# Quadrant score products, rearranged fp32 products and split first loads in a two-layer decoder step

## Chip, core and metric

One core of a Trainium2 chip runs the whole kernel. The metric is the device time of one execution in microseconds (us), lower is better. The profile shows five engines: PE (TensorE: matmul, with PEld for its weight loads), DVE (VectorE), ACT (ScalarE), POOL (GpSimd) and SP (the queue that issues the DMAs).

## What is computed

One inference step of a two-layer decoder trunk on a prompt of 2048 tokens (width 1024) and on 8 single tokens ("samples"). Layer 0 has a gated linear recurrence (RG-LRU) and layer 1 a sliding-window attention with 16 heads of 64 over a window of 128 keys; both have, beside it, a 4-head attention over a memory of 256 rows. Cut to what matters:

```python
mem_n = rmsnorm(mem_prompt[None], mem_norm_g[:, None, None, :])
mkv = jnp.einsum('lbmd,lde->lbme', mem_n, w_mem_kv)          # memory K and V of both layers
for l in range(2):
    proj = rmsnorm(x, norm_g[l]) @ w_in[l]
    u, g_main, q_mem, g_mem = split(proj)
    y = rglru(causal_conv(u)) if l == 0 else sink_attend(rope(u), k_att, v_att, band_mask, sinks)
    om = mem_attend(q_mem, mem_k[l], mem_v[l])
    x = x + concat(y * silu(g_main), om * silu(g_mem)) @ w_out[l]

def band_mask(nb):                                            # of 256 keys, query qi sees 128
    qi = jnp.arange(WINDOW)[:, None] + WINDOW
    ki = jnp.arange(2 * WINDOW)[None, :]
    local = (ki <= qi) & (qi - ki < WINDOW)
```

Everything is float32. The large products are made from three products of split operands (hi*hi, hi*lo, lo*hi) in the type fp32r; small ones (memory K/V, samples, transposes, scores and values of the window attention, the gates of the recurrence) are plain fp32 matmuls, which the profile shows as two records each (transposes as one).

## The kernel before

Each engine runs a list of instructions written out by hand, and semaphores tie the lists together. The order on PE is therefore the order in the code.

**Start** (`start`). SP loads the parameters `prm`, the transposed memory `mem_T` and the samples `xs_T` (both into `mt`, semaphore `mm_ld`), then the memory's weights `w[0]` and `w[1]` (`mk_ld`), the prompt's chunk 0 once as rows (`xr`, for the sums of squares) and once as columns (`raw`), and so on. ACT scales the memory by its gain (`memory_gain`, one step for each of 8 parts k of the width), squares it and then the rows of chunk 0 (`squares`), and takes roots. DVE adds up the squares (`tree`), inverts the roots and builds diagonal matrices (`diagonal`). PE makes the memory's products `memory(i)`, i = 0 to 3 for layer 0 (16 matmuls each, two halves h times eight parts k), `memory_sums`, and the factors as products with a diagonal: `memory_spread` for the memory, `spread(c)` for chunk c of the prompt. Its order is memory 0, sums, memory 1, memory_spread, spread 0, memory 2, memory 3. DVE then normalizes the chunk (`normal`), ACT rounds it (`high`), DVE forms the rest (`low`); `evac(i)` takes the memory's products out of PSUM.

**Memory attention** (`mem_pe`, 16 items per layer: 4 heads by 4 chunks c of 512 tokens). For item q PE does two projections of 24 matmuls (`project` for query and gate, line 569), the transposes of the item before (`mem_flip`, line 649), the scores (`mem_scores`, line 674), the values of the item before (`mem_values`, lines 661 and 664); in an item with c = 1 the samples' projection (`project_samples`, line 589, 8 matmuls with 32 stationary columns), and in layer 0's items 2, 6, 10 and 14 the memory's products 4 to 7 of layer 1 (`end`, which calls `memory`, line 414). The weights of `memory(4)` are loaded by `load_second` once `spread(3)` of item 2 is done.

**Recurrence** (`lru_pe`, 32 items): project, gates of the item before (`lru_gates`, line 861: four 64x64 matmuls on the four quadrants of the array), project, and with q % 4 = 1 the samples' projection.

**Window attention** (`swa_pe`, 32 items): project, transposes of item q-2 (`swa_flip`, line 1096), scores of item q-1 (`swa_scores`, line 1112: 8 matmuls, for four tiles t of 128 queries and two heads h; head h lies in partitions 64h to 64h+63), project, values of item q-2 (`swa_values`, line 1123), with q % 4 = 0 the samples' projection. ACT copies the second 128 keys' scores to `X`; DVE replaces the columns k > q of `X` by those of the first 128 keys (`swa_max`, by the predicate `pick`), so of the 256 scores of a query 128 are used.

**Output projection** (`output`, line 1970) follows in each layer.

Of the kernel before, what the change touches and what calls it, by code (L numbers as in the profile page):

```python
# [8 lines left out]
ACT = mybir.ActivationFunctionType  # L9
# [4 lines left out]
KT = D // 128  # L14
# [11 lines left out]
M = 256  # L26
# [118 lines left out]
def start(nc, m, sem, A, outs):  # L145
# [3 lines left out]
    prm_ld, sink_ld, ids, soft, exp_r = (sem("su_" + s) for s in ("prm", "sink", "ids", "soft", "exp"))  # L149
    mm_ld, mm_g, mm_sq, mm_add, mm_sum, mm_rt, mm_dg, mm_bc, mm_xs = (sem("mm_" + s) for s in ("ld", "g", "sq", "add", "sum", "rt", "dg", "bc", "xs"))  # L150
    mk_ld = [sem(f"mk_ld{i}") for i in range(8)]
    mk_kt = [sem(f"mk_kt{p}") for p in range(2)]
    mk_done, mk_ev, mk_st = (sem("mk_" + s) for s in ("done", "ev", "st"))
    x_ld, r_ld = ([sem(f"in_{n}{c}") for c in range(NCH)] for n in ("ld", "rows"))
# [36 lines left out]
    def sync(s, item_weights):  # L191
        def load_rows(c):
            s.dma_start(xr[c][:, :, :], A["x_prompt"][0, CH * c:CH * c + CH].rearrange("(t p) d -> p t d", p=128)).then_inc(r_ld[c], 16)

        def load_columns(c):
            s.dma_start(raw[c][:, :, :], A["x_T"][c]).then_inc(x_ld[c], 16)

        def load_x(c):
            load_rows(c)
            load_columns(c)  # L200

        def load_w(i):
            s.dma_start(w[i][:, :, :], A["w_mem_kv"][i]).then_inc(mk_ld[i], 16)

        s.dma_start(m.prm[:, :, :], A["prm"]).then_inc(prm_ld, 16)
        s.dma_start(mt[:, :, 0:M], A["mem_T"]).then_inc(mm_ld, 16)
        s.dma_start(mt[:, :, M:NM], A["xs_T"]).then_inc(mm_ld, 16)
        load_w(0)
        load_w(1)
        load_x(0)  # L210
        load_w(2)
        load_w(3)
        item_weights(s, 0)
        load_x(1)
        load_x(2)
        item_weights(s, 1)

        s.wait_ge(mk_done, 2)
        load_rows(3)
        s.wait_ge(mk_done, 4)  # L220
        load_columns(3)
        s.dma_start(m.sink_bc[:, :], A["sinks"].broadcast_to([128, NH])).then_inc(sink_ld, 16)
        for b in range(NS):
            s.dma_start(m.sink_col[b * NH:(b + 1) * NH, :], A["sinks"].rearrange("a h -> h a")).then_inc(sink_ld, 16)
        for i in range(4):
            store(s, i)
# [53 lines left out]
            nc.scalar.activation(m.hi[c][:, half(h), :], raw[c][:, half(h), :], ACT.Copy).then_inc(x_hi, 1)  # L280

    def scalar(act, first_weights):
        def memory_gain(l):
            for k in range(KT):
                nc.scalar.activation(mg[l][k][:, :], mt[:, k, 0:M], ACT.Copy, scale=m.prm[:, k, R_MG + l:R_MG + l + 1]).then_inc(mm_g, 1)

        act.wait_ge(prm_ld, 16)
        act.wait_ge(mm_ld, 32)
        memory_gain(0)
        nc.scalar.activation(sqm[:, :, :], mt[:, :, :], ACT.Square).then_inc(mm_sq, 1)  # L290
        act.wait_ge(ids, 2)
        squares(act, 0)
        act.wait_ge(mm_sum, 1)
        nc.scalar.activation(st[:, 12:14], sums_m[:, 0:2], ACT.Sqrt, bias=m.eps, scale=1.0 / D)
        nc.scalar.activation(st[0:NS, 14:15], sums_m[0:NS, 2:3], ACT.Sqrt, bias=m.eps[0:NS, :], scale=1.0 / D).then_inc(mm_rt, 1)
        memory_gain(1)
        high(act, 0)
        first_weights(act)
        squares(act, 1)
# [39 lines left out]
    def vector(v, c, first_weights):  # L339
        v.wait_ge(mm_sq, 1)  # L340
        tree(v, c, sqm, mm_add)
        v.wait_ge(ids, 8)
        c.link(nc.vector.tensor_tensor(m.twin[:, :], m.ident[:, 0:NS], m.ident[:, NS:2 * NS], ALU.add))
        for j in range(1, 4):
            c.link(nc.vector.tensor_tensor(m.twin[:, :], m.twin[:, :], m.ident[:, 32 * j:32 * j + NS], ALU.add))
        diagonal(v, c, 0)
        v.wait_ge(mm_rt, 1)
        c.link(nc.vector.reciprocal(st[0:NS, 18:19], st[0:NS, 14:15]))
        c.link(nc.vector.reciprocal(rows_m, st[:, 12:14]))
        nc.vector.tensor_tensor(dgm[0:NS, 2, 0:NS], m.ident[0:NS, 0:NS], st[0:NS, 18:19].broadcast_to([NS, NS]), ALU.mult)  # L350
        nc.vector.tensor_tensor(dgm[:, 0:2, :], m.ident[:, :].unsqueeze(1).broadcast_to([128, 2, 128]), bc(rows_m, 128), ALU.mult).then_inc(mm_dg, 1)
        normal(v, 0)
        v.wait_ge(mm_bc, 1)
        c.link(nc.vector.tensor_copy(rbm[:, :], factor_m))
        evac(v, 0)
        evac(v, 1)
        low(v, 0)
        evac(v, 2)
        first_weights(v)

        y = mt[:, :, M:NM]
        c.link(nc.vector.tensor_tensor(y, y, rbm[:, M:NM].unsqueeze(1).broadcast_to([128, KT, NS]), ALU.mult))
        c.link(nc.vector.tensor_copy(m.xs[:, :, 0:NS], y))
        nc.vector.tensor_tensor(m.xs[:, :, NS:2 * NS], y, m.xs[:, :, 0:NS].bitcast(F32), ALU.subtract)
        nc.vector.tensor_tensor(m.xsg[:, :, 0:NS], y, bc(m.prm[:, :, R_G], NS), ALU.mult).then_inc(mm_xs, 1)
        diagonal(v, c, 1)
        evac(v, 3)
# [34 lines left out]

    def memory(pe, i):
        l = i // 4
        pe.wait_ge(mk_ld[i], 16)
        if i >= 4:
            pe.wait_ge(mk_ev, i)
        for h in range(2):
            for k in range(KT):
                if h == 0 and i % 4 == 0:  # L410
                    pe.wait_ge(mm_g, KT * l + k + 1)
                a, b = w[i][:, k, :], mg[l][k][:, :]
                s_, r_ = (a[:, 128 * h:128 * h + 128], b) if is_k(i) else (b[:, 128 * h:128 * h + 128], a)
                last = nc.tensor.matmul(mk_bank(i)[:, 256 * h:256 * h + 256], s_, r_, start=(k == 0), stop=(k == KT - 1))  # L414
        last.then_inc(mk_done, 1)

    def tensor(pe):
        def memory_sums():
            pe.wait_ge(mm_add, 1)
            for t in range(3):  # L420
                n = 128 if t < 2 else NS
                last = nc.tensor.matmul(m.bank[2][0:n, 8 * t:8 * t + 8], sqm[:, 0, 128 * t:128 * t + n], ones[:, 0:8], start=True, stop=True)
            last.then_inc(mm_sum, 1)

        def memory_spread():
            pe.wait_ge(mm_dg, 1)
            nc.tensor.matmul(factor_m[:, 0:M], ones[:, :], dgm[:, 0:2, :].rearrange("p t c -> p (t c)"), start=True, stop=True)
            nc.tensor.matmul(factor_m[:, M:NM], ones[0:NS, :], dgm[0:NS, 2, 0:NS], start=True, stop=True).then_inc(mm_bc, 1)

        pe.wait_ge(ids, 1)  # L430
        memory(pe, 0)
        memory_sums()
        memory(pe, 1)
        memory_spread()
        spread(pe, 0)
        memory(pe, 2)
        memory(pe, 3)

    return dict(exponential=exponential, sync=sync, pool=pool, scalar=scalar, vector=vector, softplus=softplus, softplus_in=softplus_in, tensor=tensor,
# [4 lines left out]
def items(nc, m, sem, l, A, st, prior=None):  # L444
# [300 lines left out]
    def mem_pe(pe, ready=None, within=None, values=None, samples=None, end=None):  # L745
        for q, (i, p, c) in enumerate(MEM):
            project(pe, "mem", i, p, 0, c, ready if q < NCH else None)
            if within:
                within(pe, q)
            project(pe, "mem", i, p, 1, c)  # L750
            if q:
                mem_flip(pe, *MEM[q - 1])
            mem_scores(pe, i, p, c)
            if q:
                if values:
                    values(pe, q)
                mem_values(pe, *MEM[q - 1])
            if q == 0 and l == 0:
                project_samples(pe, "mem", 0)
            if c == 1:  # L760
                if samples:
                    samples(pe, q)
                of_samples(project_samples, pe, "mem", i, p)
            if end:
                end(pe, q)

    def mem_act(act, within, behind=None, flipped=None):
        for q, (i, p, c) in enumerate(MEM):
# [96 lines left out]
    def lru_pe(pe, tail):  # L865
        for q in range(NL + 1):
# [6 lines left out]
            else:  # L873
                tail(pe)
                lru_gates(pe, q - 1)
            if q < NL:
                project(pe, "main", *LRU[q][:2], 1, q % 4)
            if q == 0:
                mem_values(pe, *MEM[-1])
            if q < NL and q % 4 == 1:  # L880
                of_samples(project_samples, pe, "main", *LRU[q][:2])

    def lru_tanh(act, chn, q):
        i, p, c = LRU[q]
# [214 lines left out]
    def swa_scores(pe, q):  # L1099
# [4 lines left out]
        else:  # L1104
# [2 lines left out]
            pe.wait_ge(S["zeros"], B["zeros"] + 2)  # L1107
            pe.wait_ge(S["k_ready"], B["k_ready"] + NCH)
            pe.wait_ge(S["v_ready"], B["v_ready"] + NCH)
        for t in range(4):  # L1110
            for h in range(2):
                last = nc.tensor.matmul(m.bank[2 + 2 * h + t // 2][:, (t % 2) * 256:(t % 2 + 1) * 256],  # L1112
                                        qf[q % 2][64 * h:64 * h + 64, t * 128:(t + 1) * 128],
                                        kT[64 * h:64 * h + 64, (4 * c + t) * 128:(4 * c + t + 2) * 128], start=True, stop=True)
        last.then_inc(S["s_done"], 1)

    def swa_values(pe, q):
# [1224 lines left out]
```

## Time and profile before

| | |
|---|---|
| time, median of 3 runs | 2135.05 us (2134.81 to 2135.98) |
| time of the profiled execution | 2137.04 us |
| its span, first to last instruction | 2135.1 us |
| PE busy | 2110.6 us, 99% of the span |
| DVE busy | 1148.2 us, 54% |
| ACT busy | 924.2 us, 43% |
| DMA, mean over the span | 94 GB/s; 388 GB/s in the first fortieth |
| PE in `project` (line 569), output (line 1970) | 48% and 23% of the chain that ended last |

The chain that ended last is followed back from the last instruction, at each step to what released it. Busy time of PE counts an instruction from its start to its modelled end, so that it also covers short stalls inside it; what a block costs is better read from the distance of starts in the chain.

### The profile page before, as it was taken

What the parts mean: (1) busy time and instruction counts of PE and PEld (TensorE: products, weight loads), DVE (VectorE), ACT (ScalarE), POOL (GpSimd) and SP (SyncE); (2) the same over time, 40 slices, a digit from 0 to 9 for tenths busy, and PEclk for the clock granted to TensorE, in tenths of its full rate; (3) what the DMA queues carried; (4) which work ended last, traced back from release to release, by engine and by line L of the source; (5) the groups of instructions that cost most, each with busy time, mean ns of one, the idle gap of its engine ahead of it and who ended that gap; (6) DMA issues with size and microseconds to landing.
All of it is one profiled execution on the core that took longest, in us unless ns stands there. A gap on an engine that the chain in (4) does not pass through costs nothing.

```text
span 2135.1 us, 28239 instructions
## 1 busy us (share of the span) xinstructions
PE 2110.6 (99%) x11357; PEld 1690.5 (79%) x11357; DVE 1148.2 (54%) x2016; ACT 924.2 (43%) x2012; POOL 26.8 (1%) x30
## 2 busy tenths in 40 slices
PE   7999999999999999999999999999999999999998
PEld 6788887777777787888788888888888888787886
DVE  4745436777767722222644544777767777723222
ACT  5633335777777732222533333444444344322111
POOL 0000000000000000000400000000000000000000
PEclk9999999999999999999999999999999999999999
DMA  9311111111112565243111102221222214475331
GB/s 388 121 62 40 67 54 49 45 49 44 49 44 71 178 205 172 93 125 108 63 35 37 43 35 65 75 67 48 77 73 68 65 58 134 132 271 174 104 104 56
DMA packets 114521, 199.91 MB, mean 94 GB/s; under 512 B 12252, under 2 KB 66844, under 8 KB 109392
## 3 DMA queue, kind: packets, MB, share of 16 engines
q1 hardware_dynamic: 114392, 198.13, 27.7%
q8 instruction: 89, 1.46, 0.3%
q14 instruction: 40, 0.33, 0.0%
HBM read 149.68 MB, written 48.48 MB: 93 GB/s over the span
## 4 chain that ended last, share of the span: by engine, by line
PE 91%; DVE 4%; ACT 2%; DMA 1%; issue 0%; SPq 0%; DVEq 0%
PE bank L569 48%; PE bank L1970 23%; PE bank L1112 3%; PE bank L1123 3%; PE bank L414 3%; PE bank L674 2%; PE bank L861 1%; PE bank L1096 1%; PE bank L661 1%; PE bank L649 1%; PE bank L589 1%; PE bank L664 1%; PE bank L1958 1%; DVE in_x L323 1%; DVE wo_lo L1712 1%; PE bank L1433 0%
## 5 line engine op out<-in xcount | busy, mean ns | idle before, releaser
L569 PE MATMUL bank<-x_hi,w_hi 128*128 128x512 f32 x1600 | 638.8, 399 | 1.2 <-ACT it_kraw L619 1.2
L569 PE MATMUL bank<-x_hi,w_lo 128*128 128x512 f32 x1600 | 624.1, 390 | 0.0
L569 PE MATMUL bank<-x_lo,w_hi 128*128 128x512 f32 x1600 | 623.4, 390 | 0.0
L569 PEld LDWEIGHTS bank<-x_hi,w_hi 128*128 128x128 f32 x1600 | 300.1, 188 | 110.4 <-issue 49.5
L569 PEld LDWEIGHTS bank<-x_hi,w_lo 128*128 128x128 f32 x1600 | 300.3, 188 | 64.7
L569 PEld LDWEIGHTS bank<-x_lo,w_hi 128*128 128x128 f32 x1600 | 300.6, 188 | 59.9 <-issue 0.7
L1970 PE MATMUL bank<-wo_hi,z_hi 128*128 128x512 f32 x768 | 303.1, 395 | 2.1 <-DVE z_lo L1741 2.1
L1970 PE MATMUL bank<-wo_hi,z_lo 128*128 128x512 f32 x768 | 299.2, 390 | 0.0
L1970 PE MATMUL bank<-wo_lo,z_hi 128*128 128x512 f32 x768 | 299.1, 389 | 0.0
L1970 PEld LDWEIGHTS bank<-wo_hi,z_hi 128*128 128x128 f32 x768 | 144.2, 188 | 35.3 <-DVE z_lo L1741 3.0
L1970 PEld LDWEIGHTS bank<-wo_hi,z_lo 128*128 128x128 f32 x768 | 144.2, 188 | 30.4
L1159 ACT ACTIVATE it_X<-it_X,stat 128x128 f32<-128x128 f32 x256 | 99.2, 389 | 157.3 <-DVE stat L1229 157.3
L1970 PEld LDWEIGHTS bank<-wo_lo,z_hi 128*128 128x128 f32 x768 | 144.3, 188 | 28.7
L614 ACT ACTIVATE it_gh<-bank 128x512 f32<-128x512 f32 x96 | 56.8, 592 | 173.3 <-PE bank L569 173.3
L720 DVE TENSOR_TENSOR it_P_lo<-bank,it_P_hi 128x512 fp32r<-128x512 f32 x64 | 41.2, 687 | 161.1 <-ACT it_P_hi L715 161.1
L1741 DVE TENSOR_TENSOR z_lo<-z_raw,z_hi 128x1536 fp32r<-128x1536 f32 x32 | 56.2, 1758 | 101.1 <-ACT z_hi L1737 101.1
L1195 DVE TENSOR_TENSOR it_PTs<-bank,tmask 128x512 f32<-128x512 f32 x128 | 79.5, 684 | 54.7 <-PE bank L1096 54.7
L1907 ACT ACTIVATE op_y<-op_x 128x1024 f32<-128x1024 f32 (+1 forms) x18 | 19.1, 1059 | 192.9 <-DVE op_x L1927 192.9
L1737 ACT ACTIVATE z_hi<-z_raw 128x1536 fp32r<-128x1536 f32 x32 | 47.6, 1487 | 98.8 <-DMA z_raw<-z_scratch 98.8
L709 ACT ACTIVATE it_Pm<-bank,stat 128x256 f32<-128x256 f32 x128 | 58.9, 474 | 70.6 <-DVE stat L727 70.5
L1927 DVE TENSOR_TENSOR op_x<-op_x,bank 128x512 f32<-128x512 f32 (+1 forms) x36 | 24.5, 685 | 114.2 <-PE bank L1970 114.1
L547 ACT ACTIVATE w_hi<-w_raw,prm 128x256 fp32r<-128x256 f32 x200 | 85.0, 506 | 0.3 <-PE bank L664 0.3
(308 smaller groups left out, 2694.6 us busy)
## 6 DMA issues: line engine op xcount, KB each, us to landing
w_raw<-in_w_items SPq DMA_DIRECT2D x25, 1024.0 KB, 5.0
z_scratch<-it_gz SPq DMA_DIRECT2D x96, 256.0 KB, 2.5
z_raw<-z_scratch SPq DMA_DIRECT2D x32, 768.0 KB, 5.7
it_cs<-in_rope SPq DMA_DIRECT2D x32, 512.0 KB, 4.2
wo_raw<-in_w_out SPq DMA_DIRECT2D x6, 2048.0 KB, 9.0
mk_w<-in_w_mem_kv SPq DMA_DIRECT2D x8, 1024.0 KB, 7.0
in_rows<-in_x_prompt SPq DMA_DIRECT2D x4, 2048.0 KB, 28.9
in_x<-in_x_T SPq DMA_DIRECT2D x4, 2048.0 KB, 26.5
```

The costliest lines, as they stand in the source:

```text
L414: last = nc.tensor.matmul(mk_bank(i)[:, 256 * h:256 * h + 256], s_, r_, start=(k == 0), stop=(k == KT - 1))
L547: nc.scalar.activation(m.w_hi[w % 2][:, k, :], m.w_raw[w % 2][:, k, :], ACT.Copy, scale=m.prm[:, k, gain(w):gain(w) + 1]).then_inc(S["w_hi ...
L569: last = nc.tensor.matmul(ps, s_, r_, start=(k == 0 and q == 0), stop=(k == KT - 1 and q == 2))
L614: nc.scalar.activation(gh[:, :], PG, ACT.Copy, scale=0.5)
L709: nc.scalar.activation(Pm[:, t, :], (S0, S1)[t // 2][:, (t % 2) * M:(t % 2 + 1) * M], ACT.Exp, bias=negm[:, t:t + 1], scale=MEM_SCALE, acc ...
L1112: last = nc.tensor.matmul(m.bank[2 + 2 * h + t // 2][:, (t % 2) * 256:(t % 2 + 1) * 256], qf[q % 2][64 * h:64 * h + 64, t * 128:(t + 1) * ...
L1123: last = nc.tensor.matmul(T0[64 * h:64 * h + 64, t * 128:(t + 1) * 128], kV[:, 4 * c + t + kt, 64 * h:64 * h + 64], PTs[:, h, kt, t * 128: ...
L1159: e = nc.scalar.activation(X[:, j, :], X[:, j, :], ACT.Exp, bias=negm[:, j:j + 1], accum_out=rs[:, j:j + 1])
L1195: r = nc.vector.tensor_tensor(PTs[:, h, a, :].rearrange("p (t k) -> p t k", t=4), (T0, T1)[h].rearrange("p (t k) -> p t k", t=4), m.tmask[ ...
L1737: nc.scalar.activation(m.z_hi[slot(t)][:, :, :], m.z_raw[slot(t)][:, :, :], ACT.Copy).then_inc(zhi, 1)
L1741: nc.vector.tensor_tensor(m.z_lo[slot(t)][:, :, :], m.z_raw[slot(t)][:, :, :], m.z_hi[slot(t)][:, :, :].bitcast(F32), ALU.subtract).then_i ...
L1970: last = nc.tensor.matmul(bank(t, h)[0:128 if t < TT else 40, :], s_, r_, start=(first and q == 0), stop=(end and q == len(pairs) - 1))
```

## The change

The window scores are cut in four: the 128 queries of a tile become two halves r, each multiplied with the 192 keys that it can see, so that 16 matmuls of 64 stationary and 192 moving columns stand in place of 8 of 128 and 256, on the quadrants (rows of head h, columns of half r). In the memory attention the samples' projection (in layer 0 from item 5 on) and `end` stand directly behind the transposes, ahead of the scores. In the recurrence the samples' projection stands behind the gates, ahead of the gate's projection. At the start the first loads are cut in halves of k, `xs_T` is loaded behind `w[0]`, ACT issues one small activation before it waits for data and scales the first four k when their half is there; PE does memory 0, memory 1, sums, spread 0, memory 2, memory_spread, memory 3; DVE does `low(0)` before it takes over the memory's factors.

```diff
--- before.py
+++ after.py
@@ -149,6 +149,8 @@
     prm_ld, sink_ld, ids, soft, exp_r = (sem("su_" + s) for s in ("prm", "sink", "ids", "soft", "exp"))
     mm_ld, mm_g, mm_sq, mm_add, mm_sum, mm_rt, mm_dg, mm_bc, mm_xs = (sem("mm_" + s) for s in ("ld", "g", "sq", "add", "sum", "rt", "dg", "bc", "xs"))
     mk_ld = [sem(f"mk_ld{i}") for i in range(8)]
+
+    mm_ld0, first_half = sem("mm_ld0"), mk_ld[4]
     mk_kt = [sem(f"mk_kt{p}") for p in range(2)]
     mk_done, mk_ev, mk_st = (sem("mk_" + s) for s in ("done", "ev", "st"))
     x_ld, r_ld = ([sem(f"in_{n}{c}") for c in range(NCH)] for n in ("ld", "rows"))
@@ -203,9 +205,11 @@
             s.dma_start(w[i][:, :, :], A["w_mem_kv"][i]).then_inc(mk_ld[i], 16)
 
         s.dma_start(m.prm[:, :, :], A["prm"]).then_inc(prm_ld, 16)
-        s.dma_start(mt[:, :, 0:M], A["mem_T"]).then_inc(mm_ld, 16)
+        s.dma_start(mt[:, half(0), 0:M], A["mem_T"][:, half(0)]).then_inc(mm_ld0, 16)
+        s.dma_start(w[0][:, half(0), :], A["w_mem_kv"][0][:, half(0)]).then_inc(first_half, 16)
+        s.dma_start(mt[:, half(1), 0:M], A["mem_T"][:, half(1)]).then_inc(mm_ld, 16)
+        s.dma_start(w[0][:, half(1), :], A["w_mem_kv"][0][:, half(1)]).then_inc(mk_ld[0], 16)
         s.dma_start(mt[:, :, M:NM], A["xs_T"]).then_inc(mm_ld, 16)
-        load_w(0)
         load_w(1)
         load_x(0)
         load_w(2)
@@ -280,13 +284,17 @@
             nc.scalar.activation(m.hi[c][:, half(h), :], raw[c][:, half(h), :], ACT.Copy).then_inc(x_hi, 1)
 
     def scalar(act, first_weights):
-        def memory_gain(l):
-            for k in range(KT):
+        def memory_gain(l, ks=range(KT)):
+            for k in ks:
                 nc.scalar.activation(mg[l][k][:, :], mt[:, k, 0:M], ACT.Copy, scale=m.prm[:, k, R_MG + l:R_MG + l + 1]).then_inc(mm_g, 1)
 
+        act.wait_ge(ids, 2)
+        nc.scalar.activation(st[:, 63:64], m.eps, ACT.Copy)
         act.wait_ge(prm_ld, 16)
+        act.wait_ge(mm_ld0, 16)
+        memory_gain(0, range(0, 4))
         act.wait_ge(mm_ld, 32)
-        memory_gain(0)
+        memory_gain(0, range(4, KT))
         nc.scalar.activation(sqm[:, :, :], mt[:, :, :], ACT.Square).then_inc(mm_sq, 1)
         act.wait_ge(ids, 2)
         squares(act, 0)
@@ -350,11 +358,11 @@
         nc.vector.tensor_tensor(dgm[0:NS, 2, 0:NS], m.ident[0:NS, 0:NS], st[0:NS, 18:19].broadcast_to([NS, NS]), ALU.mult)
         nc.vector.tensor_tensor(dgm[:, 0:2, :], m.ident[:, :].unsqueeze(1).broadcast_to([128, 2, 128]), bc(rows_m, 128), ALU.mult).then_inc(mm_dg, 1)
         normal(v, 0)
+        low(v, 0)
         v.wait_ge(mm_bc, 1)
         c.link(nc.vector.tensor_copy(rbm[:, :], factor_m))
         evac(v, 0)
         evac(v, 1)
-        low(v, 0)
         evac(v, 2)
         first_weights(v)
 
@@ -402,11 +410,14 @@
 
     def memory(pe, i):
         l = i // 4
-        pe.wait_ge(mk_ld[i], 16)
+        if i:
+            pe.wait_ge(mk_ld[i], 32 if i == 4 else 16)
         if i >= 4:
             pe.wait_ge(mk_ev, i)
         for h in range(2):
             for k in range(KT):
+                if i == 0 and h == 0 and k % 4 == 0:
+                    pe.wait_ge((first_half, mk_ld[0])[k // 4], 16)
                 if h == 0 and i % 4 == 0:
                     pe.wait_ge(mm_g, KT * l + k + 1)
                 a, b = w[i][:, k, :], mg[l][k][:, :]
@@ -429,11 +440,11 @@
 
         pe.wait_ge(ids, 1)
         memory(pe, 0)
+        memory(pe, 1)
         memory_sums()
-        memory(pe, 1)
-        memory_spread()
         spread(pe, 0)
         memory(pe, 2)
+        memory_spread()
         memory(pe, 3)
 
     return dict(exponential=exponential, sync=sync, pool=pool, scalar=scalar, vector=vector, softplus=softplus, softplus_in=softplus_in, tensor=tensor,
@@ -750,6 +761,14 @@
             project(pe, "mem", i, p, 1, c)
             if q:
                 mem_flip(pe, *MEM[q - 1])
+
+            beside = c == 1 and (l == 1 or q > 1)
+            if beside:
+                if samples:
+                    samples(pe, q)
+                of_samples(project_samples, pe, "mem", i, p)
+            if end:
+                end(pe, q)
             mem_scores(pe, i, p, c)
             if q:
                 if values:
@@ -757,12 +776,10 @@
                 mem_values(pe, *MEM[q - 1])
             if q == 0 and l == 0:
                 project_samples(pe, "mem", 0)
-            if c == 1:
+            if c == 1 and not beside:
                 if samples:
                     samples(pe, q)
                 of_samples(project_samples, pe, "mem", i, p)
-            if end:
-                end(pe, q)
 
     def mem_act(act, within, behind=None, flipped=None):
         for q, (i, p, c) in enumerate(MEM):
@@ -873,12 +890,12 @@
             else:
                 tail(pe)
                 lru_gates(pe, q - 1)
+            if q < NL and q % 4 == 1:
+                of_samples(project_samples, pe, "main", *LRU[q][:2])
             if q < NL:
                 project(pe, "main", *LRU[q][:2], 1, q % 4)
             if q == 0:
                 mem_values(pe, *MEM[-1])
-            if q < NL and q % 4 == 1:
-                of_samples(project_samples, pe, "main", *LRU[q][:2])
 
     def lru_tanh(act, chn, q):
         i, p, c = LRU[q]
@@ -1107,11 +1124,14 @@
             pe.wait_ge(S["zeros"], B["zeros"] + 2)
             pe.wait_ge(S["k_ready"], B["k_ready"] + NCH)
             pe.wait_ge(S["v_ready"], B["v_ready"] + NCH)
+
         for t in range(4):
-            for h in range(2):
-                last = nc.tensor.matmul(m.bank[2 + 2 * h + t // 2][:, (t % 2) * 256:(t % 2 + 1) * 256],
-                                        qf[q % 2][64 * h:64 * h + 64, t * 128:(t + 1) * 128],
-                                        kT[64 * h:64 * h + 64, (4 * c + t) * 128:(4 * c + t + 2) * 128], start=True, stop=True)
+            for r in range(2):
+                for h in range(2):
+                    o, e = 128 * t + 64 * r, 64 * r
+                    last = nc.tensor.matmul(m.bank[2 + 2 * h + t // 2][e:e + 64, (t % 2) * 256 + e:(t % 2) * 256 + e + 192],
+                                            qf[q % 2][64 * h:64 * h + 64, o:o + 64],
+                                            kT[64 * h:64 * h + 64, (4 * c + t) * 128 + e:(4 * c + t) * 128 + e + 192], start=True, stop=True)
         last.then_inc(S["s_done"], 1)
 
     def swa_values(pe, q):
```

## Rows read from the trace of the kernel before

**Rows 1.** The page: busy time, share of the span, instructions by engine.

```profile
PE 2110.6 (99%) x11357; PEld 1690.5 (79%) x11357; DVE 1148.2 (54%) x2016; ACT 924.2 (43%) x2012; POOL 26.8 (1%) x30
```

**Rows 2.** Waits of PE: total us, times, longest.

```profile
PE bank L661 <- ACT it_P_hi L715: 2.0, 1, 2.0
```

**Rows 3.** Chain in order of time, the start: start us, us, engine, line.

```profile
10.79 8.70 PE bank L414 x32
...
19.97 7.10 PE bank L414 x32
...
27.82 1.06 PE bank L401 x2
28.88 13.81 PE bank L414 x64
```

**Rows 4.** Timeline of the start: start us, us, engine, line, operation, tiles.

```profile
18.38 1.06 ACT L271 ACTIVATE in_rows<-in_rows 128x1024 f32<-128x1024 f32 x1 [3.66 <-DMA in_rows<-in_x_prompt]
...
24.57 0.69 DVE L317 TENSOR_TENSOR in_diag<-ident,stat 128x512 f32<-128x512 f32 x1
...
34.98 4.48 DVE L329 TENSOR_TENSOR x_lo<-in_x,x_hi 128x2048 fp32r<-128x2048 f32 x2
```

**Rows 5.** Timeline of PE, transposes of memory item 2.

```profile
86.60 1.03 PE L649 MATMUL bank<-ident,it_Pm 128*128 128x128 f32 x8
```

**Rows 6.** Chain, end of item 2 and item 3 of layer 0's memory attention.

```profile
93.00 8.39 PE bank L414 x32
101.39 10.93 PE bank L569 x48
112.31 0.87 PE bank L649 x8
113.19 1.44 PE bank L674 x12
...
116.02 10.93 PE bank L569 x48
```

**Rows 7.** Busy time by stretch; granted TensorE clock is the third value from the end.

```profile
93.00:94.00 1.00, 1.00 (x3) 0.80 (x3) 1.00 (x1) 0.98 (x3) 0.00 (x0) 0.50 0.00 0
```

**Rows 8.** SP's queue: the load for memory product 4; its tile's times to landing.

```profile
81.31 0.34 SPq L246 DMA_DIRECT2D mk_w<-in_w_mem_kv  x1
...
DMA to landing us min/median/max: 5.3/7.0/20.6
```

**Rows 9.** Chain, layer 0's memory attention, a memory product of layer 1.

```profile
227.69 6.91 PE bank L414 x32
```

**Rows 10.** Chain, recurrence: an item without and one with the samples' projection.

```profile
374.20 11.12 PE bank L569 x48
385.32 1.02 PE bank L861 x8
...
392.02 1.00 PE bank L589 x16
...
398.73 1.02 PE bank L861 x8
```

**Rows 11.** Timeline of the weight loads, one item's gates in the recurrence.

```profile
385.25 0.21 PEld L861 LDWEIGHTS bank<-it_uc,it_bd 64*64 64x64 f32 x8 [0.35 <-issue]
```

**Rows 12.** Chain, window attention: an item with and one without the samples' projection.

```profile
1440.11 0.87 PE bank L1096 x8
1440.98 1.93 PE bank L1112 x16
...
1448.59 1.90 PE bank L1123 x32
...
1457.16 0.87 PE bank L1096 x8
...
1473.19 0.87 PE bank L1096 x8
```

**Rows 13.** Timeline of DVE, window attention: the item's last step before its transposes.

```profile
1470.43 1.23 DVE L1239 TENSOR_TENSOR it_X<-it_X,stat 128x1024 f32<-128x1024 f32 x1
```

## The prediction

> **What bounds the kernel now.** I read the page first, then PE's waits, then the chain in order of time, and last single stretches of the timelines. The reader is to see that PE is busy 2110.6 of 2135.1 us [rows 1], so outside the first 10.8 us some 14 us of idle time are left, and that the one stall with a place in this change is 2.0 us before the values of memory item 1, in item 2 [rows 2]. In the chain PE follows PE: block behind block, each costing the distance to the next start. So time is won where a PE block gets shorter, where two neighbouring blocks meet at a cheaper seam, or where PE starts its unbroken run earlier. I cost each part in PE time and then ask whether DVE, ACT or a load becomes late.
>
> **1. Quartered scores (the largest term).** The block of 8 matmuls costs 1.93 us [rows 12]. Its two heads run side by side in two row halves: in one lane 4 matmuls of 256 columns in fp32 at four passes, 4 x 256 x 4 / 2.4 GHz = 1.71 us; 0.22 us are the seam (first weight load and draining). New: 16 matmuls of 192 columns. If all four quadrants run at once, a lane again has 4 matmuls, now 4 x 192 x 4 / 2.4 = 1.28 us. The nearest row is the recurrence's gates: four 64x64 fp32 matmuls of 512 columns, one in each quadrant, cost 1.02 us together [rows 10], where one lane alone needs 512 x 4 / 2.4 = 0.85 and four behind one another 3.41. So quadrants do run four abreast, with a seam of 0.17; and that kernel form also writes both row halves into one bank, which the new scores don't. The window's values, 16 matmuls in two column halves with different moving data, show 1.90 against 1.71 [rows 12], a seam of 0.19. New block: 1.28 + 0.17 to 0.22 = 1.45 to 1.50. Saved 0.43 to 0.48, I take 0.47; 32 items: **15.0 us** (13.8 to 15.4).
>
> Could the weight loads bind? There are now 32 load records of 64 columns an item for 16 of 128. Transposes, one load of 128 columns each, go at 0.87 / 8 = 0.109 us [rows 6], so 64 columns cost about 0.054 and 32 of them in a single row 1.74 us: that would eat the whole gain. But in the gates 8 such loads lie within 0.21 us, the last one's latency included [rows 11], where a single row needs 0.43. Loads of different quadrants overlap. Even if only the two row halves did, a lane's step needs 2 x 0.054 = 0.11 us of loading beside 192 x 2 / 2.4 = 0.16 of streaming.
>
> The rule that speaks against this part is of the Trainium skill ("TensorE: Matmul & The Clock Gate", section "The mechanism" of Part 3): a weight load overlaps a running matmul only if its row group differs. The two query halves share a row group, so by it they would take turns. The rows on gates and values contradict it (above); what it would give is rival B.
>
> Who gets late? The critical way from one item's transposes to the next leads through DVE and ACT and ends with DVE's normalization at 1470.43 + 1.23 = 1471.66, the next transposes start at 1473.19 [rows 12, 13]: 1.5 us of room, of which the shorter block takes 0.47. It hides behind PE. The predicate discards all columns that are no longer computed, so ACT and DVE do what they did.
>
> **2. Samples behind the gates.** An item of the recurrence without samples is 11.12 + 1.02 = 12.14 us long, one with them from 386.34 (end of the gates) to 399.75, 13.41 [rows 10]: they cost 1.27, between two full-array blocks. In the window attention they follow the values, already a tiled block: an item with them is 1457.16 - 1440.11 = 17.05, one without 1473.19 - 1457.16 = 16.03 [rows 12], cost 1.02. The change puts them behind the tiled gates, so 0.25 saved in each of 7 items (the eighth of this phase has no next weights): **1.75 us** (0 to 2). The weights that they read are loaded from the item with q % 4 = 0 on; they are now wanted 5.6 us earlier, still over 17 us after that item's start, against 5.3 to 7.0 for a load of this size [rows 8]. The Trainium skill ("TensorEngine Tiling (Array Packing)", section "Key Properties") says that a change of tiling mode drains TensorE; by it one of four changes goes here, and the trace agrees (1.27 against 1.02).
>
> **3. Samples and memory products ahead of the scores.** 7 samples blocks (layer 0 items 5, 9, 13; layer 1 items 1, 5, 9, 13) and memory products 5 to 7 now follow the transposes. These run on the full array. A memory product at full clock costs 6.91 us, 32 x 0.216, between the fp32r values and an fp32r projection [rows 9], which is 32 halves of 256 x 4 / 2.4: changing between fp32 and fp32r has no seam there. For the samples the number of tiled stretches stays the same. I take **0**; bounds: 0.25 won at each of 10 (2.5) and 0.1 lost at each of 7 (0.7). The scores come later, but behind them still lie the values and two projections before the next transposes, 116.02 - 113.19 - 1.44 + 10.93 = 12.3 us, exactly what items without samples have today [rows 6], and those don't wait. The end of the K/V stage in layer 1's item 0 moves likewise, at 0; its inputs are from before that item's two projections.
>
> **4. Memory product 4 ahead of item 2's scores.** Here the stall of 2.0 us goes: PE waits for ACT's `P_hi` [rows 2], which in ACT's list stands behind the rounding of chunk 3. Now 6.9 us of products lie in front of that wait. Before: transposes at 86.60, item 3 at 101.39, a distance of 14.8 [rows 5, 6]. After: 0.87 + 6.91 + 1.44 + 1.40 (116.02 less 114.63) = 10.6. Gain 4.2. It contains a second effect: after the stall the granted clock was 0.50, that is 1.2 of 2.4 GHz [rows 7], and the product took 8.39 against 6.91 [rows 6, 9], 1.5 us. No stall, no drop. The product's weights are issued at 81.31 and land 5.3 to 7.0 us later, 86.6 to 88.3 [rows 8], the transposes end at 87.5: on time, or up to 0.8 late. I take **4.0** (3.4 to 4.2; 2.5 if the clock drops all the same).
>
> **5. Start.** Before, PE runs unbroken from 10.79 to 42.69, the end of memory 3 [rows 3]. After, `spread(0)` stands after memory 1 and the sums; its diagonal is done at 24.57 + 0.69 = 25.3, bound by the rows of chunk 0, whose squares begin at 18.38 when they land [rows 4]; the loads ahead of them keep their bytes, so 25.3 stays. From there: about 0.1 of reaction, 1.06 (spread) + 6.91 + 0.75 (memory_spread, 27.82 - 27.07) + 6.91 = 41.05. Gain **1.6**. Is PE at `spread(0)` by 25.3? The gains of k 4 to 7 wait for `mm_ld`, now complete only with `xs_T` behind `w[0]`, whose bytes were there at 10.7; by then 4 of 16 products are done. The other 12 take 5.2, memory 1 6.9, sums 0.5 [rows 3, 9]: 23.8 with full clock, 25.6 if the 1.8 us that memory 0 lost (8.70 against 6.91) are lost again. Gain 1.2 to 1.6. DVE's new order: normal and low take 4.5 us each [rows 4], so low(0) ends near 26.5 + 9 = 35.5; the factors' copy, three evacuations and the first of the weights' rests follow, some 3 us by my estimate: 38.5, 2.5 before PE wants it. Four more issues of SP (some 0.5 us each) hide behind a full DMA queue. ACT's small activation only brings its table load forward.
>
> **Sum.** 15.0 + 1.75 + 0 + 4.0 + 1.6 = 22.35. The profiled execution took 2137.04 (span 2135.1 and 1.9 around it): after, 2114.7, span 2112.75. It lay 2.0 above the median of the runs, 2135.05, so for a median **2112.7 us**, 1.05% faster.
>
> **Rivals.**
> A, the forecast, with terms inside their bounds: 2110 to 2116; chance 0.69.
> B, slower: only two quadrants run at a time because halves r of one head take turns (the page's rule, or the moving data of both coming from the same 64 partitions). 8 steps of 192 x 4 / 2.4 = 0.32 are 2.56, + 0.22 = 2.78 a block, 0.85 more in each of 32, 27.2 lost, 7.35 won: 2155. It decides from a block of 1.93 + 7.35 / 32 = 2.16 on. For it: no row has both halves of a row group with different moving data and 64 rows; against: gates and values. 0.04.
> C, weight loads bind the new block at 1.74 + 0.2: no gain there, 2135.05 - 7.35 = 2127.7. Against: rows 11. 0.04.
> D, the early part gives little: PE stands before `spread(0)` or for memory 4's weights, the clock falls to 1.2 GHz behind it (1.5 to 1.7 us a time, as measured), or the order on DVE makes item 0 or 1 late. Parts 4 and 5 then give 0 to 3 of 5.6: 2115.3 to 2118.3. For it: item 2's chain through DVE and ACT is tight already. 0.15.
> E, the moves of part 3 do save a seam, up to 2.5: 2110.2 and below. For it: the scores follow transposes today; against: the 0.216 above. 0.08.
>
> **Numbers.** 0.2% (4.3 us) is about what a measurement of this kernel can tell from no change. Faster by more: A, C, D and E, 0.96, of which 0.01 goes to "within" for several terms failing at once: 0.95. Slower: B, 0.04. Range: 2109.5 (E) to 2119 (D); it leaves out B, C and tails, 0.1 to 0.2.
>
> **What the profile after would show.** Line 1112's successor at 1.45 to 1.50 us a block with 32 records, four starting together (B: 2.8; C: 1.9); window items of 15.56 us; recurrence items with samples 13.16 instead of 13.41; no wait of PE before the values in item 2 and no clock of 0.50 near 90 us; `spread(0)` at 25.4; the first projection at 41. The prediction fails above all if the scores' block is not near 1.5, then if DVE's normalization in the window items comes later than 1 us before the transposes.

## The result and the profile after

| | before | after |
|---|---|---|
| time, median of 4 runs each | 2134.93 us (2134.72 to 2135.98) | 2114.94 us (2114.40 to 2115.23) |
| ratio, 95% interval | | 0.9905 (0.9888 to 0.9922) |
| time of the profiled execution | 2137.04 us | 2115.23 us |
| its span | 2135.1 us | 2113.4 us |

The change takes 20.0 us off the median and 21.8 off the profiled executions; 22.35 were forecast for both. The line numbers of the changed kernel are higher: `project` is line 580, the memory's products 425, the transposes of the memory attention 660, its scores 685, the samples' projection 600, the gates 878, the window's transposes 1113, scores 1132 and values 1143.

The page of the changed kernel, busy time by engine:

```profile
PE 2093.3 (99%) x11869; PEld 1680.3 (80%) x11869; DVE 1148.9 (54%) x2016; ACT 924.3 (44%) x2013; POOL 26.9 (1%) x30
```

PE stays the bound, and DVE and ACT do what they did [rows 1]. 512 more matmul records are the window's scores. The waits of PE after (total us, times, longest):

```profile
PE bank L425 <- DMA mk_w<-in_w_mem_kv: 8.0, 1, 8.0
PE bank L1990 <- DVE z_lo L1761: 2.2, 3, 0.9
PE bank L580 <- ACT it_kraw L630: 1.2, 1, 1.2
```

The wait for ACT's `P_hi` [rows 2] is gone. The chain of the changed kernel, start and first items (start us, us, engine, line):

```profile
6.63 12.22 DMA in_rows<-in_x_prompt
...
25.88 1.13 PE bank L409 x2
27.00 6.91 PE bank L425 x32
33.91 0.43 PE bank L438 x2
34.34 0.31 PE bank L439 x2
34.65 7.10 PE bank L425 x32
41.76 5.48 PE bank L580 x24
...
85.81 0.87 PE bank L660 x8
86.69 6.91 PE bank L425 x32
93.59 1.43 PE bank L685 x12
95.02 0.93 PE bank L672 x4
95.95 0.47 PE bank L675 x2
96.42 10.93 PE bank L580 x48
```

The first projection starts 0.9 us earlier than before, 41.76 for 42.69 [rows 3], item 3 starts 5.0 us earlier, 96.42 for 101.39 [rows 6]. From item 2's transposes to item 3 it is 10.6 us, as worked out, and memory product 4 takes 6.91 instead of 8.39: the granted clock does not fall. The chain now begins with the load of the rows of chunk 0, which bounds `spread(0)` at 25.88.

Now the same chain in the recurrence and in the window attention:

```profile
380.17 1.02 PE bank L878 x8
381.19 1.00 PE bank L600 x16
382.19 11.13 PE bank L580 x48
393.32 1.02 PE bank L878 x8
...
1430.08 0.87 PE bank L1113 x8
1430.95 1.46 PE bank L1132 x32
...
1438.09 1.90 PE bank L1143 x32
1439.99 1.00 PE bank L600 x16
...
1446.66 0.87 PE bank L1113 x8
1447.54 1.46 PE bank L1132 x32
...
1462.22 0.87 PE bank L1113 x8
```

An item of the recurrence with samples takes 393.32 - 380.17 = 13.15 us instead of 13.41 [rows 10]. The block of window scores takes 1.46 us instead of 1.93 [rows 12], with 32 records for 16. An item with samples takes 16.58 instead of 17.05, the next one, without them, 15.56 instead of 16.03. How the scores run is seen in the timelines of one block, the weight loads and the matmuls that begin in its first 0.07 us:

```profile
1447.46 0.21 PEld L1132 LDWEIGHTS bank<-it_kT,it_qf 64*64 64x64 f32 x8 [0.17 <-issue]
1447.47 0.39 PE L1132 MATMUL bank<-it_kT,it_qf 64*64 64x192 f32 x4
```

Four matmuls begin together and eight loads lie within 0.21 us, the picture of the gates [rows 11].

### The profile page after: what moved, and what is told of

Same layout as the page of the kernel before. It is cut to its first block, busy times and chain, and to the rows that moved or that the text cites. A ratio compares the mean times of both kernels' runs of the same rounds, so it can differ in the third digit from the quotient of the medians.

```text
span 2113.4 us, 29267 instructions
## 1 busy us (share of the span) xinstructions
PE 2093.3 (99%) x11869; PEld 1680.3 (80%) x11869; DVE 1148.9 (54%) x2016; ACT 924.3 (44%) x2013; POOL 26.9 (1%) x30
## 4 chain that ended last, share of the span: by engine, by line
PE 91%; DVE 5%; ACT 2%; DMA 1%; issue 0%; SPq 0%; DVEq 0%; ACTq 0%
PE bank L580 49%; PE bank L1990 23%; PE bank L1143 3%; PE bank L685 2%; PE bank L1132 2%; PE bank L425 2%; PE bank L878 1%; PE bank L672 1%; PE bank L1113 1%; PE bank L660 1%; PE bank L600 1%; DVE wo_lo L1732 1%; PE bank L675 1%; PE bank L1978 1%; DMA in_rows<-in_x_prompt 1%; PE bank L1453 0%
```

## The experiments

Each kernel was compared with runs of the kernel before on its own chip; the medians of before in the three groups were 2135.51 (27 runs), 2135.53 (21) and 2135.61 (11). The changed kernel's own group had 2134.93 (4 runs), 0.6 to 0.7 us lower, so a difference between its median and that of a kernel of another group is uncertain by about as much.

| kernel | median us | runs | ratio to before, 95% interval |
|---|---|---|---|
| e1_scores | 2122.14 | 5 | 0.9937 (0.9925 to 0.9950) |
| e2_ahead | 2132.99 | 11 | 0.9987 (0.9978 to 0.9996) |
| e3_gates | 2133.94 | 11 | 0.9991 (0.9982 to 0.9999) |
| e4_start | 2134.64 | 11 | 0.9996 (0.9987 to 1.0005) |
| e5_headwise | 2137.20 | 10 | 1.0009 (1.0000 to 1.0018) |
| e6_item2 | 2133.03 | 11 | 0.9988 (0.9979 to 0.9997) |
| e7_old_start | 2116.34 | 4 | 0.9913 (0.9899 to 0.9926) |
| e8_start2 | 2114.61 | 4 | 0.9903 (0.9889 to 0.9916) |
| e9_order | 2115.16 | 5 | 0.9906 (0.9892 to 0.9920) |
| e10_start3 | 2113.67 | 4 | 0.9898 (0.9884 to 0.9912) |
| e11_old_scores | 2129.63 | 8 | 0.9972 (0.9962 to 0.9983) |

### One part alone (e1_scores to e4_start)

Each is the kernel before with some hunks of the change's diff, shown in full above: e1_scores has the one of `swa_scores`, e2_ahead those of `mem_pe`, e3_gates that of `lru_pe`, e4_start those of `start`.

```diff
--- e1_scores, beside the kernel before
-            for h in range(2):
-                last = nc.tensor.matmul(m.bank[2 + 2 * h + t // 2][:, (t % 2) * 256:(t % 2 + 1) * 256],
+            for r in range(2):
+                for h in range(2):
+                    o, e = 128 * t + 64 * r, 64 * r
...
--- e2_ahead, beside the kernel before
+            beside = c == 1 and (l == 1 or q > 1)
+            if beside:
...
+            if end:
+                end(pe, q)
             mem_scores(pe, i, p, c)
...
--- e3_gates, beside the kernel before
+            if q < NL and q % 4 == 1:
+                of_samples(project_samples, pe, "main", *LRU[q][:2])
             if q < NL:
                 project(pe, "main", *LRU[q][:2], 1, q % 4)
...
--- e4_start, beside the kernel before
         pe.wait_ge(ids, 1)
         memory(pe, 0)
+        memory(pe, 1)
         memory_sums()
-        memory(pe, 1)
-        memory_spread()
         spread(pe, 0)
         memory(pe, 2)
+        memory_spread()
```

> The kernel before with the quartered scores alone. If the four quadrants run abreast as the changed kernel's trace reads (block of 1.46 us for 1.93), 32 x 0.47 = 15.0 us less: 2119.9. If part of the gain in the window attention is only there together with the other edits, or is given back at the stage's end, less: 2121 to 2123.

> The kernel before with samples and memory products ahead of the scores alone. Theory 1: the stall before item 1's values (2.2 us in the profiled execution of before) goes and nothing else, because the drop of the granted clock behind it is not in most executions of before: 2.2 to 2.5 us less, 2132.5. Theory 2: the drop is in every execution of before, 4.0 us less: 2130.9. In both no granted clock of 0.5 near 90 us in the trace of this run.

> The kernel before with the samples' projection behind the gates alone. One change of tiling mode less in 7 items at 0.26 us: 1.8 us less, 2133.1; items with samples 13.15 us long instead of 13.41. Rival: the next projection's weights or ACT come late and it gives nothing.

> The kernel before with the start alone (loads in halves, order of the products, low(0) first). If the start is worth what the two traces show, 0.9 us less: 2134.0. If the earlier start only lengthens the stall before item 1's values (that wait hangs on a chain through DVE and ACT), nothing: 2134.9, with a stall of 2.9 instead of 2.0 us. The prediction's own term was 1.6: 2133.3.

Measured: 13.4, 2.5, 1.6 and 0.9 us less than before, the last not resolved from zero. The profiled run of e1_scores (2123.95 us, the slowest of its five) has a drop of the clock late, in the output projection of layer 1. Busy time by stretch, the granted clock is the third value from the end; below it two blocks of the chain, both of 12 matmuls:

```profile
1864.00:1866.00 2.00, 2.00 (x6) 1.54 (x5) 0.00 (x0) 0.00 (x0) 0.00 (x0) 0.50 1.06 388
```

```profile
1862.39 4.44 PE bank L1973 x12
1866.84 1.24 PE bank L1436 x12
1868.07 2.87 PE bank L1973 x12
```

The slowed block costs 1.6 us more than the other. So the 13.4 are not a clean price of the scores; e11_old_scores gives one. Each execution's mean granted clock is on record with three digits: of the five, the two with 0.999 took 2120.95 and 2121.09, 14.5 us below before, and the three with 0.998 took 2122.14 to 2123.95. e2_ahead stands with theory 1: 2.5, not 4.0. Whether the drop behind item 1's stall was there differs among the profiled runs of the kernels that still have the stall:

| profiled run | granted clock behind the stall | first projection | item 3 | between |
|---|---|---|---|---|
| before | 0.5 | 42.69 | 101.39 | 58.70 |
| e3_gates | 0.5 | 42.61 | 101.31 | 58.70 |
| e1_scores | full | 43.90 | 100.93 | 57.03 |
| e4_start | full | 41.36 | 98.38 | 57.02 |
| e2_ahead (no stall) | full | 43.69 | 98.38 | 54.69 |
| after (no stall) | full | 41.76 | 96.42 | 54.66 |

The stall costs 57.03 - 54.69 = 2.3 us in each of them and the drop 1.7 where it comes, in two of four. The table corrects something else: the first projection of a kernel with the old start lies anywhere from 42.61 to 43.90, by when memory product 0 starts (10.37 to 11.14) and by how long it takes (8.68 to 9.74 us, at the lower clock for part of it). The 0.9 us between the two traces is therefore one draw. Over the profiled runs it is 43.2 on average with the old start (before, e1_scores, e2_ahead, e3_gates, and below e6_item2 43.30 and e7_old_start 42.82) and 41.7 with the new one (after, e4_start, and below 42.56, 41.57 and 41.27 of e5_headwise, e9_order and e11_old_scores): 1.5 us apart.

### Two quadrants at a time, and the order inside a tile (e5_headwise, e9_order)

Both are the changed kernel with its loops over tiles, halves and heads in another order.

```diff
--- e5_headwise, beside the changed kernel
-        for t in range(4):
-            for r in range(2):
-                for h in range(2):
+        for h in range(2):
+            for t in range(4):
+                for r in range(2):
--- e9_order, beside the changed kernel
         for t in range(4):
-            for r in range(2):
-                for h in range(2):
+            for h in range(2):
+                for r in range(2):
```

> The changed kernel with the head as the outermost loop of the scores, so that only two quadrants, the two query halves of one head, have work at any one stretch. It prices rival B, which would have had this in the change. If the matmuls run in issue order, two abreast: 8 steps of 0.32 and a seam, 2.78 us a block instead of 1.46, 32 x 1.32 = 42 us more than the changed kernel, 2157. If halves of one head take turns instead (the rule that a weight load overlaps a matmul only in another row group), 16 steps: over 5 us a block, 2230. If the queue pulled the second head's matmuls forward, 2115.

> The changed kernel with the two loops inside a tile exchanged: the two halves of one head next to each other, then the other head. With the head outermost a block took 2.16 us, less than two abreast (2.78), so PE started matmuls of the other head past waiting ones. If it can do that, the order inside a tile is free: 1.46 us a block, 2114.9. If neighbours of one head take turns at each tile, 0.16 us more at each of four tiles and 32 blocks: up to 20 us more, 2135.

e5_headwise loses the gain: it is 22.3 us slower than the changed kernel, which is 32 blocks of 0.70 us more, and 1.7 us slower than before. A block is none of those that were expected (2.78 for two abreast, over 5 for one at a time, 1.46 for four abreast). The chain of its window attention, and PE's busy time in three stretches of a block, of line 1132 alone (in brackets the records in the stretch):

```profile
1453.07 0.87 PE bank L1113 x8
1453.94 2.16 PE bank L1132 x32
1456.11 5.68 PE bank L580 x24
```

```profile
1453.88:1454.04 0.16, 0.16 (x2) 0.16 (x4) 1.00 0.00 0
...
1454.52:1454.68 0.16, 0.16 (x8) 0.14 (x8) 1.00 0.00 0
...
1455.80:1455.96 0.16, 0.16 (x4) 0.00 (x0) 1.00 0.00 0
```

At the start only two matmuls run, in the middle twice as many as at either end are in flight (a record lasts 0.32 us, so a later stretch counts two generations), at the end two run again. 4 steps with two, 4 with four and 4 with two hold 2 x 4 + 4 x 4 + 2 x 4 = 32 records in 12 steps of 0.16, 1.96 us and a seam of 0.2. The single records give the order: the first head's eight pairs start between 1453.88 and 1455.07, the second head's first pair starts at 1454.59, right behind the first head's fifth. (Which head a record belongs to is read from its place in these two rows, 0.16 us apart; the records don't name it.) PE started the second head's matmuls ahead of three pairs of records of the first, some way ahead but not far enough. Had each record waited for the one before it to start, the second head could have begun at 1455.07 at the earliest, and a block would take 2.16 + 0.48 = 2.64 us. e9_order confirms the near case: 2115.16 us, and its blocks take 1.46:

```profile
1446.52 0.87 PE bank L1113 x8
1447.39 1.46 PE bank L1132 x32
1448.85 5.68 PE bank L580 x24
```

Within a tile the order is free; over a whole head it isn't.

### Item 2 alone, and all but one part (e6_item2, e7_old_start, e11_old_scores)

e7_old_start is the change without its hunks in `start`, e11_old_scores without the one in `swa_scores` (the diffs above, left out). e6_item2 is the kernel before with

```diff
                 mem_flip(pe, *MEM[q - 1])
+            if end and q == 2:
+                end(pe, q)
             mem_scores(pe, i, p, c)
...
-            if end:
+            if end and q != 2:
                 end(pe, q)
```

> The kernel before with nothing but item 2's memory product ahead of its scores. If part 3 of the change (the other moves ahead of the scores) is worth nothing, this gives all that the moves ahead of the scores gave together: 2.5 us less than before, 2133.0. If the other ten moves were worth the 0.1 to 0.2 us each that an avoided change of type would save, this is 1 to 2 us slower than that.

> The changed kernel with the start of before: everything but the start. If the start is worth the 0.9 us of the two traces, 2115.8 beside 2114.9. If the parts alone (13.4, 2.5, 1.6, 0.9, sum 18.4) add up and the 1.6 to 2.2 us that the whole change gains on top come from the start together with the others, 2117 or more.

> The changed kernel with the scores of before. The scores alone gave 13.4 us in the median, with a drop of the granted clock near 1863 us in the profiled run (1.6 us) that the changed kernel does not show. If that drop is what was missing and the blocks are worth 15.0: 2130.0, 5 us less than before. If the scores are only worth 13.4, 2128.4, and the other parts 6.6 together instead of the 5.0 that they gave singly.

e6_item2 (2133.03) equals e2_ahead (2132.99) within what these runs can tell: the other ten moves ahead of the scores show no gain, and the 2.5 us are the stall. Why is seen in the chain of the changed kernel, in item 5 of layer 0, and in item 7 without samples:

```profile
136.61 0.87 PE bank L660 x8
137.48 1.00 PE bank L600 x16
138.49 1.63 PE bank L685 x12
...
141.51 10.93 PE bank L580 x48
...
174.84 1.44 PE bank L685 x12
```

The seam behind the samples' tiled matmuls (0.19 us) only moves from the projection to the scores, 1.63 instead of 1.44. e11_old_scores (2129.63) is 14.7 us above the changed kernel (2114.94), and 14.5 above e9_order (2115.16), which has blocks of the same 1.46 us and was timed in the same group; by each one's gain over its own runs of before it is 14.0 (20.0 less 6.0). This is the scores' price, near the 15.0 of the blocks. Without the start's hunks the changed kernel takes 1.4 us more (2116.34), against 0.9 where the start is added to the kernel before. By each one's gain over its own runs of before, the first is 0.8 (20.0 less 19.2). The medians as they stand fit the 1.5 us of the profiled runs; between these figures the start's price stays open. In e4_start the stall is still there (2.0 us in its trace), and its executions fall in two groups, four from 2133.33 to 2134.17 and seven from 2134.61 to 2135.49, with the profiled one (no drop) in the lower: the drop behind the stall would explain the higher group. The mean clocks on record speak for it: the lower four have 0.999 or 1.000, and all four executions with 0.998 lie in the upper group. None of the 61 executions of kernels without the stall has 0.998, of before 10 of 27, 3 of 21 and 2 of 11 have it. But none of e3_gates' eleven has it either, though its trace shows the drop, so three digits don't count the drops; and where in the execution the clock fell is seen in the profiled one alone. This is argued, not shown.

### A better start (e8_start2, e10_start3)

```diff
--- e8_start2, beside the changed kernel
-        s.dma_start(mt[:, :, M:NM], A["xs_T"]).then_inc(mm_ld, 16)
+        s.dma_start(mt[:, :, M:NM], A["xs_T"]).then_inc(mk_ld[5], 16)
...
-        act.wait_ge(mm_ld, 32)
+        act.wait_ge(mm_ld, 16)
         memory_gain(0, range(4, KT))
+        act.wait_ge(mk_ld[5], 16)
         nc.scalar.activation(sqm[:, :, :], mt[:, :, :], ACT.Square).then_inc(mm_sq, 1)
-        act.wait_ge(ids, 2)
+        nc.scalar.activation(st[:, 62:63], m.eps, ACT.Sqrt)
         squares(act, 0)
...
-            pe.wait_ge(mk_ld[i], 32 if i == 4 else 16)
+            pe.wait_ge(mk_ld[i], 32 if i in (4, 5) else 16)
--- e10_start3, beside e8_start2
         load_w(1)
-        load_x(0)
+        load_rows(0)
         load_w(2)
+        load_columns(0)
         load_w(3)
```

> The changed kernel with two more edits at the start: the gains of k 4 to 7 wait for their half of the memory alone and no longer for the samples' load behind the weights, and ACT takes its table load for the roots while it waits for the rows of chunk 0. If the start is now bound by PE's resuming at 11.9 us and by ACT's table load ahead of the root (1.28 us), both 1.0 to 1.3 us earlier, 1.0 to 1.2 us less than the changed kernel: 2113.8. If it is bound by the landing of the rows alone, or the second table load comes back elsewhere, 2114.9.

> The kernel with the second start (its own load for k 4 to 7, early table load for the roots) and, beside that, the third memory product's weights loaded ahead of chunk 0's columns. With the second start PE waited 0.6 us for those weights, which landed at 26.2 behind the columns. Now they land near 21, the columns near 26.2, where DVE wants them at 25.7. If PE is what bounds the start, 0.7 us less than the second start, 2113.9; if DVE's late begin (0.5 us) comes through to the first projection, 2114.6.

In e8_start2 PE runs memory 0 and 1 without a break and `spread(0)` starts at 24.48, 1.4 us earlier, but then PE waits for a load that was hidden before. Timeline of PE:

```profile
7.97 15.77 PE L426 MATMUL bank<-mm_g,mk_w 128*128 128x256 f32 x64 [7.97 <-DMA mk_w<-in_w_mem_kv]
...
26.23 6.09 PE L426 MATMUL bank<-mk_w,mm_g 128*128 128x256 f32 x27 [0.61 <-DMA mk_w<-in_w_mem_kv]
```

2114.61 us is not told apart from the changed kernel. With these weights ahead of the columns (e10_start3) the chain of the start is PE's alone, and the first projection is at 40.05:

```profile
7.64 16.02 PE bank L427 x64
23.65 0.47 PE bank L435 x6
...
24.16 1.12 PE bank L411 x2
25.29 6.91 PE bank L427 x32
...
40.05 5.47 PE bank L582 x24
```

Its four runs (2113.50 to 2113.88) all lie below the four of the changed kernel (2114.40 to 2115.23), 1.3 us between the medians; it beats both kernels by its median, though the two were not timed side by side and the intervals of their ratios overlap.

## Why the prediction was right, and where it was off

| part | forecast us | in the traces | by experiment, medians |
|---|---|---|---|
| 1 scores | 15.0 | 32 x 0.47 = 15.0 | 14.7 (e11_old_scores less after; 14.0 by own befores) |
| 2 samples behind the gates | 1.75 | 7 x 0.26 = 1.8 | 1.6 (e3_gates) |
| 3 moves ahead of the scores | 0 | 0 | 0.0 (e2_ahead less e6_item2) |
| 4 memory product 4 | 4.0 | 4.0 | 2.5 (e6_item2) |
| 5 start | 1.6 | 0.9 | 1.4 (e7_old_start less after; 0.8 by own befores), 0.9 (e4_start) |
| sum | 22.35 | 21.7 | 20.2 with the first figure of each |

**Scores: right, with the mechanism.** Four quadrants abreast, 1.28 us and a seam of 0.18. Rival C is out (1.46, not 1.9). Rival B is out: halves of one head do not take turns, neither in the changed kernel nor in e9_order. A loss of that kind comes from the same matmuls only in another order, e5_headwise's. The rule of the Trainium skill by which a weight load overlaps a running matmul only in another row group ("TensorE: Matmul & The Clock Gate", "The mechanism") does not hold here: halves of one row group load and run side by side, eight loads within 0.21 us and four matmuls at once. Another sentence of that section, that the matmuls start in strict order, is at odds with e5_headwise, where the second head's first pair starts ahead of three of the first's. The 2.78 us a block that I carried over from rival B to e5_headwise were too high, since PE began the second head early. Rival B's own 2.78 was for halves that take turns, and no run here shows that.

**Gates: right.** 13.15 us against the 13.16 named. By the Trainium skill's rule on draining ("TensorEngine Tiling (Array Packing)", "Key Properties") one drain of four goes; the trace agrees, 0.26 us.

**Moves ahead of the scores: right at zero.** Rival E is out.

**Memory product 4: right in the profiled execution, too large for the median.** The distance from transposes to item 3 was forecast at 10.6 and is 10.6, and the clock does not fall. The step that failed is in the sum: "It lay 2.0 above the median of the runs, 2135.05, so for a median 2112.7 us". I took those 2.0 us as a constant beside the change, while the profiled execution of before held a drop of 1.5 to 1.7 us that I had put into term 4. An event that only some executions have can't be paid out in full on the median: 2.5 of 4.0 came. That the traces give 4.0 and not the 4.2 worked out is a matter of two views: the 86.60 was a start in the timeline, which lies 0.16 before the same block's start in the chain (85.65 and 85.81 in the changed kernel).

**Start: the size was a little high.** `spread(0)` came at 25.88, not 25.4, since the rows of chunk 0 landed 0.5 us later (ACT takes them up at 18.93 instead of 18.38 [rows 4]; SP issued them at 6.63), and I overlooked a seam: memory 3 follows the 8-row matmuls of `memory_spread` and takes 7.10 instead of 6.91. These two make up the 0.7 us between the forecast and the traces' 0.9. That the two groups of profiled runs lie 1.5 apart, near the forecast 1.6, is partly luck: 42.69, from which I counted, was an early draw (43.2 on average), and the changed start lost 0.7 to what I had overlooked.

Of rival D nothing came in the changed kernel: PE waited 0.2 us before `spread(0)` and not for the weights of memory 4. The room on DVE shrank by what was said: in the item of [rows 12, 13] it was 1473.19 - 1471.66 = 1.5 us and is now 1462.22 - (1459.91 + 1.23) = 1.1. The window attention's first item has the least, 0.6 us by the timeline; that is under the 1 us named as a sign of failure, yet PE waits for DVE before none of these transposes.

```profile
1459.91 1.23 DVE L1259 TENSOR_TENSOR it_X<-it_X,stat 128x1024 f32<-128x1024 f32 x1
```

Left open: how often the clock drops behind item 1's stall in the kernel before, and whether that is the 1.0 us by which the parts 2 to 5 give more together (6.0, e11_old_scores) than singly (5.0).

## What to carry to other kernels

Where PE is busy without a gap, price a change by the distance of block starts in the chain: the streaming of the longest lane (columns x passes / clock) plus a seam of about 0.2 us at each change of tiling; data type alone changed nothing. A mask that zeroes a corner is worth a quarter of the product if the matmul then fits the quadrants, issued so that every four in a row use all four quadrants (in e5_headwise neighbours differ too, but only between two). And before a term goes from one profiled execution to a median, ask whether it holds an event, such as a clock drop behind a stall, that the other executions may not have.

## What the hardware showed that I had not expected

PE does not wait in line for a busy quadrant: with one head issued wholly ahead of the other, the second head's matmuls began 0.71 us into the first's, ahead of three waiting pairs, and a block took 2.16 us where starts in strict order give 2.64. The seam of a tiled block also follows a single 8-row matmul (7.10 against 6.91). The same stall of 2.0 us was followed by the granted clock of 0.50 in two profiled runs and by full clock in two others, and the start of memory product 0 took from 8.68 to 9.74 us in identical code (the old start, six traces).
